# A state-space scan stage: decay rows and their ones held on 128 partitions instead of 2

## The chip, the cores and the metric

The kernel runs as one program on 1 core of one Trainium2 chip. Its time is the device time of an execution in microseconds (us); the profile is of one execution. The engines are TensorE (PE; PEld is its weight load), VectorE (DVE), ScalarE (ACT), GpSimd (POOL) and SyncE (SP, which here issues DMAs).

## What is computed

The kernel is one layer of a diffusion backbone: four parallel branches over 1024 tokens (a conformer convolution, a bidirectional state-space scan, a Hyena branch, a short convolution), merged by gates, and then a mixture of experts. The change lies in the scan branch. Per direction, the reference works over chunks of 128 tokens with 12 heads in 4 groups:

```python
def ssd_scan(xdt, log_decay, b_in, c_out, init):
    xc, a_cum, bc = _ssd_blocks(xdt, log_decay, b_in)
    cc = c_out.reshape(bc.shape).astype(F32)
    h_in, final = _ssd_chunk_states(xc, a_cum, bc, init)
    lower = jnp.tril(jnp.ones((SSD_CHUNK, SSD_CHUNK), dtype=bool))
    decay_in = jnp.exp(jnp.where(lower, a_cum[..., :, None] - a_cum[..., None, :], -jnp.inf))
    cb = jnp.einsum("bclgn,bcsgn->bgcls", cc, bc.astype(F32))
    y_diag = jnp.einsum("bgcls,bgecls,bcsgep->bclgep", cb, decay_in, xc.astype(F32))
    y_off = jnp.einsum("bclgn,cbgepn,bgecl->bclgep", cc, h_in, jnp.exp(a_cum))
    return (y_diag + y_off).reshape(xdt.shape).astype(xdt.dtype), final
```

The two directions are added, with a skip term `xs * ssd_d`. What the change touches is `decay_in`: for every chunk, head and direction a 128x128 table of exp(difference of two cumulated log decays), with one triangle left out.

## The kernel before, in words

`build_program` runs the stages one after another, with a barrier of all engines between them. `stage_scan` has a part of its own for every engine; inside it each engine runs its list in order, and waits on semaphores only. The stage has two parts.

- The early part goes through 11 steps (`early`). In each, SP loads `xs` and `b_tok`, POOL scales them (`ending`, L1346), PE makes a chunk state of four products of 128x192 (`chunk_state`, L1379), and DVE updates the running state (L1491, L1494).
- The loop goes through the 8 chunks, last to first, for both directions together. A chunk has six units `u` of two heads. For each unit PE runs `segments(n, u)`: for either direction a product of the unit matrix `eye` with the table `never` (0, or -1e30 in the forbidden triangle, L1399), and on top of it a product of `ones` with `rows` (L1400). `rows` holds the cumulated log decays in two pieces of fp32r on two partitions, so that L1400 has only 2 rows of contraction; it spreads the sum of the two pieces over all 128 output partitions. ACT takes the exponential (`grow`, L1465, four instructions a unit), and DVE adds the directions (L1501) and multiplies by the scores (L1506): `mix(n, q)`, once for each half `q` of three units.

The other work of a chunk on PE: four products of 128x128 for the scores (L1429), two sets of four of 128x192 with the states (`states_out`, L1407), two sets of six of 128x64 (`diagonal`, L1417) and the next chunk state (L1379). The order on PE in a round is L1429, L1407 (forward), units 3 and 4, L1407 (backward), unit 5, L1417 (half 0), L1379, units 0 to 2 of the next chunk, L1417 (half 1).

What waits for what in the loop: the segments use three PSUM banks in turn, so a unit waits until ACT has read the one three before it (`grown`). DVE's `take_off` (L1512) waits for L1407, and the second L1407 waits for the first L1512 (`off_read`). L1417 of half 0 waits for DVE's L1519 (`y_done`) and for `mix(n, 0)`. L1379 waits for the second L1512. DVE's L1541 waits for L1379, and `mix(n, 1)` stands behind it on DVE. L1417 of half 1 waits for `mix(n, 1)`, and behind it on PE stand L1429 and the first L1407 of the next round. POOL fetches `rows` for the next chunk by two DMAs (L1355), each when PE is done with that half; POOL also computes the skip term (L1367) and `ending`. SP loads the next chunk after `y_done`.

An fp32 product is two records in the profile (so "x8" is four products); an fp32r product is one.

Of the kernel before, what the change touches and what calls it, by code (L numbers as in the profile page):

```python
# [21 lines left out]
F32R = mybir.dt.float32r  # L22
I32 = mybir.dt.int32
ALU = mybir.AluOpType
# [3 lines left out]
P = 128  # L28
# [9 lines left out]
HEADS = 12  # L38
# [856 lines left out]
def ssd_scan_stages(k, merged):  # L895


    with ExitStack() as ctx:
        sb = k.resident(ctx)
        n = CHUNKS + CTX_CHUNKS  # L900
        dt = {name: sb("dt_" + name, [P, n, 2, HEADS]) for name in
              ("exp_cum", "dt_to_end", "total", "bias")}
        stage_ssd_project(k, dt, merged)
        stage_scan(k, dt, merged)
# [343 lines left out]
def stage_scan(k, dt, merged):  # L1248
# [6 lines left out]
    nc, a, ps = k.nc, k.a, k.ps  # L1255
    half, PAIR = SSD_D // 2, 2 * P
    FIRST = 11
    with k.stage("scan") as (sb, sem):
        b_chan, c_chan = sb("b_chan", [P, 2, GROUPS, P]), sb("c_chan", [P, 2, GROUPS, P])
        b_tok, xs = sb("b_tok", [P, 2, GROUPS * P]), sb("xs", [P, 2, SSD_D])  # L1260
        xend = sb("xend", [P, 2, SSD_D])
        rows = sb("rows", [2, 2, HEADS * P], F32R)
        eye, ones = sb("eye", [P, P], F32R), sb("ones", [2, P], F32R)
        never = sb("never", [P, 2, PAIR], F32R)
        grow_f, grow_b = sb("grow_f", [P, 2, HEADS, P]), sb("grow_b", [P, HEADS, P])
        off, skip, state_b = sb("off", [P, SSD_D]), sb("skip", [P, SSD_D]), sb("state_b", [P, 2, SSD_D])
        d_row = sb("d_row", [P, HEADS])
        d_in = sem("d_in")
        in_state, in_out = [sem("in_state0"), sem("in_state1")], [sem("in_out0"), sem("in_out1")]
        in_rows = [sem("in_rows0"), sem("in_rows1")]  # L1270
        skip_ready, rounded, xend_ready, state_mm, state_read = (sem(x) for x in (
            "skip_ready", "rounded", "xend_ready", "state_mm", "state_read"))
# [7 lines left out]
        by_chunk = a["cum_rows"].rearrange("q f (c d h) t -> q (f c) d (h t)", d=2, h=HEADS)  # L1280
        SEG = (0, 1, 7)

        def chunk(n):
            return CHUNKS - 1 - n

        def at(name, c, d, lo=0, hi=HEADS):
            return dt[name][:, c, d, lo:hi]

        def per_head(v, width=HD):
            return v.unsqueeze(2).broadcast_to([P, v.shape[1], width])  # L1290

        def heads(v):
            return v.rearrange("p (h e) -> p h e", e=HD)
# [13 lines left out]
        with nc.Block() as block:  # L1307
            @block.sync
            def _(sp):
                sp.dma_start(d_row[:, :], k.row("ssd_d")).then_inc(d_in, 16)  # L1310

                def load_state(m, c):
                    b = m % 2
                    sp.dma_start(xs[:, b, :], a["xbc_tok"][c, :, 0:SSD_D]).then_inc(in_state[b], 16)
                    sp.dma_start(b_tok[:, b, :], a["xbc_tok"][c, :, SSD_D:SSD_D + GROUPS * P]).then_inc(in_state[b], 16)

                def load_out(n):
                    c = chunk(n)
                    for q, dst in enumerate((b_chan, c_chan)):
                        src = a["xbc_chan"][GROUPS * q:GROUPS * (q + 1), :, c * P:(c + 1) * P]  # L1320
                        sp.dma_start(dst[:, n % 2, :, :], src.rearrange("g p t -> p g t")).then_inc(in_out[n % 2], 16)

                for m, (d, c) in enumerate(early):
                    if m >= 2:
                        sp.wait_ge(state_mm, m - 1)
                    load_state(m, c)
                    if m == 1:
                        load_out(0)
                for n in range(CHUNKS):
                    m = FIRST + n  # L1330
                    if n < 2:
                        sp.wait_ge(state_mm, m - 1)
                    else:
                        sp.wait_ge(y_done, n - 1)
                    load_state(m, chunk(n))
                    if n:
                        load_out(n)

            @block.gpsimd
            def _(pool):  # L1340
                def ending(m, c, d):

                    pool.wait_ge(in_state[m % 2], 32 * (m // 2 + 1))
                    if m >= 2:
                        pool.wait_ge(state_mm, m - 1)
                    nc.gpsimd.tensor_tensor(heads(xend[:, m % 2, :]), heads(xs[:, m % 2, :]),  # L1346
                                            per_head(at("dt_to_end", c, d)), ALU.mult).then_inc(xend_ready, 1)

                for m, (d, c) in enumerate(early):
                    ending(m, c, d)  # L1350
                def load_rows(n, q):
                    if n:
                        pool.wait_ge(seg_mm, 6 * (n - 1) + 3 * q + 3)
                    part = slice(q * half * 2, (q + 1) * half * 2)
                    pool.dma_start(rows[:, :, part], by_chunk[:, chunk(n), :, part]).then_inc(in_rows[q], 16)  # L1355

                pool.wait_ge(d_in, 16)
                load_rows(0, 0)
                load_rows(0, 1)
                for n in range(CHUNKS):  # L1360
                    m = FIRST + n
                    if n + 1 < CHUNKS:
                        load_rows(n + 1, 0)
                    pool.wait_ge(in_state[m % 2], 32 * (m // 2 + 1))
                    if n:
                        pool.wait_ge(y_begun, n)
                    nc.gpsimd.tensor_tensor(heads(skip[:, :]), heads(xs[:, m % 2, :]), per_head(d_row[:, :]),  # L1367
                                            ALU.mult).then_inc(skip_ready, 1)
                    if n + 1 < CHUNKS:
                        ending(m, chunk(n), 1)  # L1370
                        load_rows(n + 1, 1)
# [77 lines left out]
            @block.scalar  # L1449
            def _(act):  # L1450
                nc.scalar.copy(eye[:, :], k.const("ident")).then_inc(rounded, 1)
                nc.scalar.copy(ones[:, :], k.ones[0:2, :]).then_inc(rounded, 1)

                def grow(n, u):
                    act.wait_ge(seg_mm, 6 * n + u + 1)
                    if n >= 2:
                        act.wait_ge(diag_mm, 2 * (n - 2) + u // 3 + 1)
                    if n >= 1:
                        act.wait_ge(summed, 2 * (n - 1) + u // 3 + 1)
                    for d in range(2):  # L1460
                        for e in range(2):
                            h = 2 * u + e
                            dst = grow_b[:, h, :] if d else grow_f[:, n % 2, h, :]
                            at_col = d * PAIR + e * P
                            ins = nc.scalar.activation(dst, ps[:, SEG[(6 * n + u) % 3], at_col:at_col + P], ACT.Exp,  # L1465
                                                       bias=at("bias", chunk(n), d, h, h + 1))
                    ins.then_inc(grown, 1)

                for n in range(CHUNKS):
                    for u in range(6):  # L1470
                        grow(n, u)

            @block.vector
            def _(v):
                ch = Chain(v, dve)
                tt = nc.vector.tensor_tensor
                for d, kept in enumerate(("upto", "from")):
                    nc.vector.tensor_scalar(never[:, d, :].rearrange("p (e t) -> p e t", e=2),
                                            k.const(kept).unsqueeze(1).broadcast_to([P, 2, P]), 1.0, BIG, ALU.subtract,
                                            ALU.mult).then_inc(rounded, 1)  # L1480
# [1484 lines left out]
```

## Time and profile before

| | |
|---|---|
| runs | 2830.58, 2832.65, 2837.83 us; median 2832.65 |
| span of the profiled execution, first to last instruction | 2830.0 us; no other time of that execution is given |
| PE busy | 2510.7 us (89%), 11856 instructions |
| DVE, ACT, POOL busy | 1640.8, 922.9, 380.7 us |
| the scan stage | 857.4 to about 1048.8 us of the span: the early part to 910.8, the loop behind it |
| mean granted TensorE clock, whole span | 0.934 of full speed |

[...] A PE instruction's end is modelled, and consecutive ones overlap in the records, so the interval from start to start tells what one costs in a stream.

### The profile page before, as it was taken

The page shows a single profiled execution, that of the slowest core. Times are in us where ns is not written, and L with a number is a line of the kernel's source. Part 1 is how long each engine was busy: PE and PEld are TensorE (multiplying, and loading weights), DVE is VectorE, ACT ScalarE, POOL GpSimd, SP SyncE. Part 2 cuts the span into 40 slices and gives each one's busy share as a digit, 9 for nine tenths or more (in the row PEclk, how much of TensorE's full clock was granted, in tenths as well). Part 3 has the DMA queues.
Part 4 walks back from the last instruction along what each step waited for, and adds up shares of the span by engine and source line. Part 5 has one row for each costly group of instructions (what it writes and reads, how often), then busy time and mean ns, then how long its engine had stood idle before and what let it go on. Part 6 is the DMA issues. An engine that isn't in the chain of part 4 may idle for free. (4 is left out here: it accounts for less than half of the span.)

```text
span 2830.0 us, 30926 instructions
## 1 busy us (share of the span) xinstructions
PE 2510.7 (89%) x11856; PEld 2008.9 (71%) x11856; DVE 1640.8 (58%) x1613; ACT 922.9 (33%) x1066; POOL 380.7 (13%) x282
## 2 busy tenths in 40 slices
PE   7879967699995999999857999999949999999994
PEld 3338755588874778788745778787838888888881
DVE  4443379533303563332387253566768888888875
ACT  4133300233320433300000010002127777777763
POOL 3210000000003210000332300010001122212210
PEclk9989988899996889999988999999959999999997
DMA  4331144213324112111100111344259999999956
GB/s 171 122 134 45 45 150 141 81 49 99 113 68 157 52 58 73 60 47 47 45 30 30 38 38 45 131 167 159 112 218 359 368 364 365 360 364 390 388 202 241
DMA packets 91342, 433.29 MB, mean 153 GB/s; under 512 B 15864, under 2 KB 25352, under 8 KB 76522
## 3 DMA queue, kind: packets, MB, share of 16 engines
q1 hardware_dynamic: 65194, 355.71, 34.2%
q0 software_dynamic: 26048, 76.20, 7.7%
q8 instruction: 68, 1.11, 0.2%
q14 instruction: 32, 0.26, 0.0%
HBM read 399.41 MB, written 53.41 MB: 160 GB/s over the span
## 5 line engine op out<-in xcount | busy, mean ns | idle before, releaser
L360 PE MATMUL ps<-uT_upper_rest,ring_rest 128*128 128x512 f32 x1360 | 541.6, 398 | 0.0
L360 PEld LDWEIGHTS ps<-uT_upper_rest,ring_rest 128*128 128x128 f32 x1360 | 258.8, 190 | 66.1
L360 PE MATMUL ps<-uT_upper_rest,cs_upper 128*128 128x512 f32 x320 | 130.2, 407 | 55.2 <-DVE cs_val L2076 46.9
L2469 PE MATMUL ps<-ex_u_raw_rest,uT_rest 128*128 128x256 f32 x560 | 156.9, 280 | 0.0
L360 PE MATMUL ps<-uT_upper_rest,xbc_upper 128*128 128x512 f32 x336 | 136.5, 406 | 7.6 <-DVE ring_rest L782 7.6
L2467 PE MATMUL ps<-ring_rest,uT_rest 128*128 128x256 f32 (+1 forms) x416 | 135.1, 325 | 3.1 <-DVE uT_rest L2776 2.4
L360 PE MATMUL ps<-uT_rest,xbc_upper 128*128 128x512 f32 x336 | 134.9, 401 | 0.0
L2467 PE MATMUL ps<-ex_upper,uT_rest 128*128 128x256 f32 (+1 forms) x424 | 134.9, 318 | 0.0
L2468 PE MATMUL ps<-ex_upper,uT_rest 128*128 128x256 f32 (+1 forms) x424 | 134.0, 316 | 0.0
L2468 PE MATMUL ps<-ring_rest,uT_rest 128*128 128x256 f32 (+1 forms) x416 | 133.2, 320 | 0.0
L2366 POOL DMA_INDIRECT y_rows<-sb_uT,ex_scatter_at x35 | 92.6, 2645 | 300.2 <-ACT sb_uT L2575 300.2
L2090 DVE SCALAR_TENSOR_TENSOR sb_y_aT<-cs_val,sb_cols,sb_y_aT 128x64 f32 (+14 forms) x120 | 117.1, 975 | 20.1 <-DVE sb_y_aT L2090 11.7
L360 PE MATMUL ps<-uT_rest,cs_upper 128*128 128x512 f32 x320 | 128.7, 402 | 0.0
L360 PEld LDWEIGHTS ps<-uT_upper_rest,cs_upper 128*128 128x128 f32 x320 | 61.4, 192 | 71.8 <-DVE cs_val L2076 47.4
L2469 PE MATMUL ps<-uT_upper_rest,uT_rest 128*128 128x512 f32 x280 | 110.8, 396 | 0.0
L2469 PE MATMUL ps<-merged_rest,ex_hid_up 128*128 128x512 f32 x280 | 110.8, 396 | 0.0
L2469 PEld LDWEIGHTS ps<-ex_u_raw_rest,uT_rest 128*128 128x128 f32 x560 | 105.3, 188 | 0.0
L1822 PE MATMUL ps<-sb_merged,ring 128*128 128x256 f32 x256 | 64.6, 419 | 34.1 <-DVE sb_merged L1917 34.1
L360 PE MATMUL ps<-uT_upper_rest,hp_upper 128*128 128x512 f32 x192 | 78.3, 408 | 15.8 <-DVE ring_rest L782 15.8
L1986 POOL TENSOR_TENSOR cs_upper<-ring,sb_ones 128x1024 fp32r<-128x1024 f32 x20 | 40.4, 2018 | 380.9 <-POOLq L348 199.7
L2467 PEld LDWEIGHTS ps<-ring_rest,uT_rest 128*128 128x128 f32 x416 | 78.9, 190 | 15.3 <-DVE uT_upper_rest L2625 6.5
L2625 DVE TENSOR_TENSOR uT_upper_rest<-sb_spare,ring_rest 128x2048 fp32r<-128x2048 f32 x36 | 80.9, 2289 | 9.9 <-ACT ring_rest L2552 9.9
(468 smaller groups left out, 6243.6 us busy)
## 6 DMA issues: line engine op xcount, KB each, us to landing
sb_spare<-in_ex_g SPq DMA_DIRECT2D x35, 2048.0 KB
ex_u_raw<-in_ex_u SPq DMA_DIRECT2D x35, 2048.0 KB, 10.4
sb_merged<-in_ex_d SPq DMA_DIRECT2D x35, 2048.0 KB
ring<-in_conv SPq DMA_DIRECT2D x32, 512.0 KB, 3.3
ring<-in_w_gate SPq DMA_DIRECT2D x32, 512.0 KB, 3.3
md_piece<-in_w_late POOLq DMA_DIRECT2D x32, 512.0 KB, 5.1
ring<-in_w_ssd SPq DMA_DIRECT2D x21, 512.0 KB, 3.2
ring<-in_w_mod SPq DMA_DIRECT2D x16, 512.0 KB, 3.3
```

The lines of the kernel that those rows point to most:

```text
L360: last = self.nc.tensor.matmul(out, weight, x[:, k, lo:hi], start=(k == 0 and n == 0), stop=(k == kt - 1 and n == 2))
L1822: mm = nc.tensor.matmul(ps[:, 4 + r, half(mt)], ring.buf[:, slot, at * P:(at + 1) * P], wave[:, h, kt, r, comp, :], start=(kt == 0 and com ...
L1986: ch.step(nc.gpsimd.tensor_tensor(upper[:, slot % 2, :], ring.buf[:, slot, :], k.ones[:, 0:1].broadcast_to([P, KT * P]), ALU.mult))
L2090: ins = nc.vector.scalar_tensor_tensor(out=acc[:, lo:hi], in0=val[:, b, lo + s * GRID_W:hi + s * GRID_W], scalar=tap(i), in1=acc[:, lo:hi] ...
L2366: pool.indirect_dma_start(out=a["y_rows"], out_offset=bass.IndirectOffsetOnAxis(scatter_at[:, i:i + 1], 0), in_=y, in_offset=None, bounds_ ...
L2467: nc.tensor.matmul(out, left_up, w_up, start=first, stop=False)
L2468: nc.tensor.matmul(out, left_lo, w_up, start=False, stop=False)
L2469: return nc.tensor.matmul(out, left_up, w_lo, start=False, stop=last)
L2625: nc.vector.tensor_tensor(chunk(rest, m, b), chunk(raw, m, b), slot(m, b).bitcast(F32), ALU.subtract).then_inc(whole, 1)
```

## The change

`rows` and `ones` get 128 partitions instead of 2. `rows` is written once with zeros by DVE, as its first instruction in the stage (0 times a broadcast of ones, 128x3072 elements). POOL's first DMA into `rows` waits for that (`blank`). The DMAs write the same two partitions as before, so the other 126 stay zero. ACT rounds `ones` on 128 partitions. The products of L1400 are written in the same way, and now contract over 128 rows, of which 126 are zero in the moving operand.

```diff
-        rows = sb("rows", [2, 2, HEADS * P], F32R)
-        eye, ones = sb("eye", [P, P], F32R), sb("ones", [2, P], F32R)
+        rows = sb("rows", [P, 2, HEADS * P], F32R)
+        eye, ones = sb("eye", [P, P], F32R), sb("ones", [P, P], F32R)
...
-        d_in = sem("d_in")
+        d_in, blank = sem("d_in"), sem("blank")
...
-                    pool.dma_start(rows[:, :, part], by_chunk[:, chunk(n), :, part]).then_inc(in_rows[q], 16)
+                    pool.dma_start(rows[0:2, :, part], by_chunk[:, chunk(n), :, part]).then_inc(in_rows[q], 16)
 
                 pool.wait_ge(d_in, 16)
+                pool.wait_ge(blank, 1)
                 load_rows(0, 0)
                 load_rows(0, 1)
...
-                nc.scalar.copy(ones[:, :], k.ones[0:2, :]).then_inc(rounded, 1)
+                nc.scalar.copy(ones[:, :], k.ones[:, :]).then_inc(rounded, 1)
...
                 ch = Chain(v, dve)
                 tt = nc.vector.tensor_tensor
+                nc.vector.tensor_scalar(rows[:, :, :].rearrange("p d (h t) -> p (d h) t", t=P),
+                                        k.ones[:, :].unsqueeze(1).broadcast_to([P, 2 * HEADS, P]), 0.0, None,
+                                        ALU.mult).then_inc(blank, 1)
                 for d, kept in enumerate(("upto", "from")):
```

DVE's list where the stage begins, before the change (the branch is the stage's first entry, `scan_never` the table that is built there, L1486 the first read of a chunk state):

```order
L1473 UNCONDITIONAL_BRANCH
L1478 TENSOR_SCALAR scan_never<-sb_consts 128x256 x2
L1486 COPY sb_merged<-ps 128x768
L1486 COPY scan_state_b<-ps 128x768
L1491 TENSOR_TENSOR sb_merged<-sb_merged,sb_dt_total 128x768
```

And after it, with line numbers higher by 1 to 4:

```order
L1474 UNCONDITIONAL_BRANCH
L1478 TENSOR_SCALAR scan_rows<-sb_ones 128x3072
L1482 TENSOR_SCALAR scan_never<-sb_consts 128x256 x2
L1490 COPY sb_merged<-ps 128x768
L1490 COPY scan_state_b<-ps 128x768
L1495 TENSOR_TENSOR sb_merged<-sb_merged,sb_dt_total 128x768
```

One instruction has come in ahead of the two that build the table. PE has the same instructions in the same order; POOL has the same ones too, its first DMA into `rows` with one wait more.

## Rows read from the trace of the kernel before

**Rows 1.** Page, head.

```profile
span 2830.0 us, 30926 instructions
```

**Rows 2.** Stretches: busy us (instructions) of PE, PEld, DVE, ACT, POOL; PEclk, DMA share, GB/s.

```profile
922.40:1036.10 113.70, 113.70 (x559) 91.22 (x559) 67.97 (x75) 47.89 (x168) 26.39 (x26) 0.91 0.22 65
929.20:932.70 3.50, 3.50 (x14) 2.10 (x12) 2.96 (x4) 1.90 (x7) 0.00 (x0) 0.99 0.00 0
932.70:939.50 6.80, 6.80 (x28) 6.44 (x28) 0.69 (x1) 1.52 (x6) 3.46 (x3) 0.50 0.01 3
983.80:987.20 3.40, 3.40 (x16) 3.40 (x16) 0.00 (x0) 0.25 (x1) 2.85 (x2) 0.50 0.02 4
```

**Rows 3.** Line L1400: durations in ns min/median/max, first and last start, form.

```profile
L1400 PE MATMUL ps<-scan_rows,scan_ones x96: 377/380/578, 911.3 to 1040.8; 2*128 2x256 f32 x96
```

**Rows 4.** PE in order of time, one round at full clock: start, us, what.

```profile
1011.01 1.52 PE L1379 MATMUL ps<-scan_xend,scan_b_tok 128*128 128x192 f32 x8
1012.23 0.41 PE L1399 MATMUL ps<-scan_never,scan_eye 128*128 128x256 f32 x1
1012.58 0.38 PE L1400 MATMUL ps<-scan_rows,scan_ones 2*128 2x256 f32 x1
1012.89 0.38 PE L1399 MATMUL ps<-scan_never,scan_eye 128*128 128x256 f32 x1
...
1016.00 1.55 PE L1417 MATMUL ps<-scan_xs,scan_grow_f 128*128 128x64 f32 x12
1017.39 1.11 PE L1429 MATMUL ps<-scan_c_chan,scan_b_chan 128*128 128x128 f32 x8
1018.34 1.47 PE L1407 MATMUL ps<-sb_merged,scan_c_chan 128*128 128x192 f32 x8
```

**Rows 5.** PE in order of time in the experts' stage.

```profile
2156.51 0.28 PE L2469 MATMUL ps<-ex_u_raw_rest,uT_rest 128*128 128x256 f32 x1
2156.63 0.28 PE L2467 MATMUL ps<-ex_upper,uT_rest 128*128 128x256 f32 x1
```

**Rows 6.** DVE in order of time, the same round as rows 4.

```profile
1004.89 0.96 DVE L1512 TENSOR_TENSOR scan_off<-ps,sb_dt_exp_cum 128x768 f32<-128x768 f32 x1 [5.18 <-PE ps L1407]
...
1007.62 0.95 DVE L1519 TENSOR_TENSOR sb_merged<-sb_merged,ps 128x768 f32<-128x768 f32 x1
...
1009.47 0.96 DVE L1512 TENSOR_TENSOR scan_off<-ps,sb_dt_exp_cum 128x768 f32<-128x768 f32 x1
...
1012.64 0.95 DVE L1541 TENSOR_TENSOR scan_state_b<-scan_state_b,ps 128x768 f32<-128x768 f32 x1 [1.22 <-PE ps L1379]
...
1014.49 0.95 DVE L1506 TENSOR_TENSOR scan_grow_f<-scan_grow_f,ps 128x768 f32<-128x768 f32 x1
...
1019.84 0.96 DVE L1512 TENSOR_TENSOR scan_off<-ps,sb_dt_exp_cum 128x768 f32<-128x768 f32 x1 [3.52 <-PE ps L1407]
```

**Rows 7.** PE in order of time at half clock, and its first segment product.

```profile
910.80 0.58 PE L1399 MATMUL ps<-scan_never,scan_eye 128*128 128x256 f32 x1 [1.12 <-DVE sb_merged L1494]
...
916.92 2.08 PE L1429 MATMUL ps<-scan_c_chan,scan_b_chan 128*128 128x128 f32 x8
918.79 2.77 PE L1407 MATMUL ps<-sb_merged,scan_c_chan 128*128 128x192 f32 x8
...
933.35 2.82 PE L1417 MATMUL ps<-scan_xs,scan_grow_f 128*128 128x64 f32 x12
935.96 2.02 PE L1429 MATMUL ps<-scan_c_chan,scan_b_chan 128*128 128x128 f32 x8
```

**Rows 8.** DVE: the first L1512 of the first and of the last chunk.

```profile
921.59 0.96 DVE L1512 TENSOR_TENSOR scan_off<-ps,sb_dt_exp_cum 128x768 f32<-128x768 f32 x1 [9.74 <-PE ps L1407]
...
1036.49 0.96 DVE L1512 TENSOR_TENSOR scan_off<-ps,sb_dt_exp_cum 128x768 f32<-128x768 f32 x1 [6.09 <-PE ps L1407]
```

**Rows 9.** DVE where the stage begins.

```profile
857.49 0.50 DVE L1478 TENSOR_SCALAR scan_never<-sb_consts 128x256 fp32r<-128x256 f32 x2 [33.77 <-PEq L348]
867.37 0.96 DVE L1486 COPY sb_merged<-ps 128x768 f32<-128x768 f32 x1 [9.38 <-PE ps L1379]
```

## The prediction

> **What bounds the kernel now.** I read the table of stretches over the scan stage first, then PE and DVE in order of time through one round of the loop, then the line of the changed product. The stages run one after another behind barriers, so the stage is judged by itself, and what it gains comes off the total. In the stretch from 922.4 to 1036.1 us PE is busy for all of 113.70 us, and DVE for 67.97, ACT for 47.89 and POOL for 26.39 [rows 2]. The loop is PE's.
>
> Two things there are odd. The first is the clock. It is 0.91 in the mean over that stretch, though PE never stops: it drops to 0.50 for 3.4 or 6.8 us at a time, for instance from 932.7 and from 983.8. The 3.5 us ahead of the first drop hold nothing but segment products, back to back, at 0.99 [rows 2]. The second is the price of a segment product. They start 0.35 and 0.31 us apart at full clock, and last 0.38 us [rows 3, 4]. In the experts' stage, products of the same form on all 128 rows (256 columns, one record each, other weights for each) start 0.12 us apart and last 0.28 us [rows 5]. The only difference in form is that L1399 and L1400 alternate between 128 rows and 2. [...]
>
> From first L1512 of the first chunk to that of the last are 114.90 us for 7 rounds, or 16.41 us each [rows 8]; a round at full clock takes 14.95 us [rows 6]. So the drops cost about 1.46 us a round, 10 us in all.
>
> **The change, part by part.**
>
> *The zeroing.* One DVE instruction of 3072 elements per partition. Two of 256 take 0.50 us [rows 9], at 0.25 to 0.29 us each, so 12 times that is 3.0 to 3.5 us. DVE has been idle there and next has work at 867.37, when `never` was done at 857.99: 9.4 us of cover [rows 9]. POOL's new wait stands ahead of its first DMA into `rows`, needed by the product at 910.80 [rows 7], some 50 us later. Cost zero; if it were not covered, 3.5 us once. ACT's copy on 128 partitions instead of 2 has the same number of elements per partition: zero.
>
> *The segment products, at full clock.* From 0.31 to 0.12 us each. Twelve of them stand before the first L1429, at half clock: 916.92 less 910.80 is 6.1 us, 0.51 each [rows 7]. At twice 0.12 they take 2.9 us. ACT is not in the way, since L1429 doesn't wait for it. That gives 3.3 us once (3.2 or a little more).
>
> In a round there are 24 of them, 7.5 us, which become 2.9. The 4.6 us are not all won, for PE then waits for DVE. PE's own work in a round becomes 2.9 + 2 x 1.39 (L1417) + 0.95 (L1429) + 1.22 (L1379) + 2 x 1.2 (L1407, the form of L1379) = 10.2 us [rows 4]. The chain that then closes the round, with each step from a row and 0.05 us for passing on a wait (an L1407 ends at 1019.81 and L1512 starts at 1019.84):
> - DVE starts L1506 of half 1 at 0, and it ends at 0.95 [rows 6]. Now PE waits for it, which it didn't before; L1417 starts at 1.01.
> - L1417 takes 1.39, L1429 0.95; L1407 starts at 3.35 [rows 4].
> - From L1407's start to L1512's are 1.50 [rows 4, 6]: 4.85.
> - L1512 to the second L1512 on DVE: 4.58 [rows 6]: 9.43. It ends at 10.39; PE starts L1379 at 10.45. (L1417 of half 0 starts after L1519, which begins 2.73 after the first L1512, ends at 8.53, and lets L1417 end by 9.99: 0.46 of slack.)
> - L1379's start to L1541's: 1.63 [rows 4, 6]: 12.08. L1541 to the next L1506: 1.85 [rows 6]: 13.93.
>
> So a round takes 13.93 us at full clock: DVE's operations and PE's by turns. The segments are hidden in it: units 0 to 2 follow L1379, units 3 and 4 lie under L1512, unit 5 under L1501 to L1519. PE waits some 3.7 us a round. ACT's work is 48 us over 7 rounds, under 7 each [rows 2]. The last chunk has no L1379 and no next units, and its end is a row of DVE operations; it stays.
>
> *The clock.* If it never fell, the sum would be 3.3 + 7 x (16.41 - 13.93) = 20.7 us. At half clock everything on PE doubles: a round is then PE's own, 20.4 us (L1417 took 2.61 to the next start and L1429 2.02, twice the value at full clock [rows 4, 7]). With a share s of the loop at half clock the gain is 20.7 - 7 x 6.5 x s. Now s is 0.18 (0.91 in the mean [rows 2]). With that s it is 12.5. Two things pull on s. The drops came behind stretches rich in 2-row products, which suggests that a product on 2 rows hardly counts as activity, and they are gone; but PE now also waits four times a round, for up to 1.8 us, and has fewer columns to stream per us. I take s as it is. Since part of any half-clock time falls on segments with slack around them (1.0 and 1.8 us a round), I take 15, between 12.5 and 20.7 and nearer the lower.
>
> [...]
>
> **Sum.** The profiled execution's span is 2830.0 us [rows 1], 2.65 under the median of 2832.65. 2830.0 - 15 = 2815.0, so 2817.6 as a median of runs.
>
> **Rivals.**
> - *Only the clock is mended.* The 0.31 us have another cause (the fp32r form with these operands), but full-row products keep the clock up. For it: the drops at full PE business. Against: the 0.12 us of the experts' products. Rounds of 14.95: 7 x 1.46 = 10.2, and perhaps 1 to 3 at the start: 2821.
> - *The clock never falls.* The chain of 13.93 with s = 0: 2832.65 - 20.7 = 2812.
> - *Nothing.* The products keep their interval and the clock its drops, since 126 zero rows are no activity, or since the small products of L1417 are what lets it fall. For it: drops also followed stretches with L1417 in them. 2832.65.
> - *Slower: the clock stays down.* PE now idles in each round; before, in the loop, it never did. If the half clock holds for over 20.7 / 45.5 = 45% of the loop, the gain is gone. At two thirds it is 7 x 6.5 x 0.67 - 20.7 = 9.6 us slower: 2842. For it: in the early part, where PE waits most, the clock falls again and again. [...] Against: at half clock PE fills the round by itself (20.4 us) and has no waits left, which is how the clock came back in every case above.
>
> **How the numbers follow.** The likeliest is the new interval with a clock that still falls at times: 0.62, 2817.6, own range 2810 to 2825. The clock alone 0.10, clock never down 0.12, nothing 0.10, slower 0.06. The three runs differ by 7 us, and whatever follows the stage meets the clock's changes at other moments, so 3 to 4 us of scatter lie on each. A measurement can tell about 0.3%, 8.5 us. Faster by that: 0.85 of the likeliest, all of "never down", 0.7 of "clock alone": 0.72. Same: 0.20. Slower: 0.06, with 0.02 for scatter. The range goes from 2808 to 2830: it leaves out the slower case, half of "nothing", and the tails, some 0.18.
>
> **What would show it.** [...] DVE's first L1516 (L1512 before) of the first chunk 3 us earlier relative to the first segment product. Rounds of 13.9 us where the clock is 1.00, with PE waiting for DVE at L1417, L1408 and L1380; if rounds are longer at full clock, I have missed a wait (ACT's `grown`, or the DMA into `rows`). The share of half clock in the loop decides between 2812, 2818 and slower. The zeroing should be over before 862 with nothing behind it late. The prediction is wrong if DVE's operations get slower beside other traffic, or if PE's waits let the clock fall for most of the loop.

## The result and the profile after

| | before | after |
|---|---|---|
| median of 4 runs each, timed side by side | 2834.45 us | 2815.98 us |
| ratio after to before, 95% interval | | 0.9939 [0.9926, 0.9953] |
| span of the profiled execution | 2830.0 us | 2816.3 us |

The gain is 18.5 us by the medians and 13.7 by the two profiled executions; the interval of the ratio is 13 to 21 us. Part of the 18.5 is scatter of the kernel before: its median in a later series of 29 runs on one chip is 2831.6 us. The profiled executions show the gain inside the scan stage. From DVE's first instruction there to the end of its last (0.95 us long) are 857.49 to 1048.82 us before [rows 9 for the begin] and 856.79 to 1033.64 after, which is 14.5 us less.

The rows of the changed kernel follow in the order of those before: the head of the page (against rows 1), the loop from the first chunk's first L1516 to the last chunk's (against rows 2), one stretch of it at half clock, and the changed product (against rows 3).

```profile
span 2816.3 us, 30928 instructions
```

```profile
916.40:1021.20 104.80, 87.36 (x563) 82.31 (x562) 83.54 (x76) 45.72 (x168) 27.29 (x27) 0.92 0.23 70
```

```profile
935.20:938.60 3.40, 3.40 (x13) 3.40 (x14) 1.38 (x2) 0.00 (x0) 0.00 (x0) 0.50 0.90 295
```

```profile
L1401 PE MATMUL ps<-scan_rows,scan_ones x96: 276/282/420, 911.0 to 1023.9; 128*128 128x256 f32 x96
```

PE no longer fills the loop (87.36 of 104.80 us busy), a product on 128 rows lasts 0.28 us instead of 0.38, and the clock still falls: 0.92 in the mean, in five stretches of about 3.4 us. PE in order of time in a round at full clock (against rows 4):

```profile
965.92 1.57 PE L1380 MATMUL ps<-scan_xend,scan_b_tok 128*128 128x192 f32 x8 [0.31 <-DVE scan_off L1516]
967.19 0.41 PE L1400 MATMUL ps<-scan_never,scan_eye 128*128 128x256 f32 x1
967.44 0.28 PE L1401 MATMUL ps<-scan_rows,scan_ones 128*128 128x256 f32 x1
967.56 0.28 PE L1400 MATMUL ps<-scan_never,scan_eye 128*128 128x256 f32 x1
...
970.46 1.55 PE L1418 MATMUL ps<-scan_xs,scan_grow_f 128*128 128x64 f32 x12 [1.54 <-DVE scan_grow_f L1510]
971.85 1.11 PE L1430 MATMUL ps<-scan_c_chan,scan_b_chan 128*128 128x128 f32 x8
972.80 1.47 PE L1408 MATMUL ps<-sb_merged,scan_c_chan 128*128 128x192 f32 x8
```

The interval is 0.12 us. PE now waits where the chain said: 1.54 us for L1510, 0.31 for the second L1516. What has gone is about as long as a weight load. Before, the load of L1400 lasts 0.18 us, starts at 1013.20 together with its own product, and the next load starts only 0.31 us after it; after, a load of 0.19 us starts every 0.12 us, 0.12 ahead of its own product, beside the products before it. First the kernel before, then the one after:

```profile
1013.20 0.18 PEld L1400 LDWEIGHTS ps<-scan_rows,scan_ones 2*128 2x128 f32 x1
1013.51 0.19 PEld L1399 LDWEIGHTS ps<-scan_never,scan_eye 128*128 128x128 f32 x1
```

```profile
967.56 0.19 PEld L1401 LDWEIGHTS ps<-scan_rows,scan_ones 128*128 128x128 f32 x1
967.68 0.19 PEld L1400 LDWEIGHTS ps<-scan_never,scan_eye 128*128 128x128 f32 x1
```

DVE in the same round, then its first and last first-L1516 (against rows 6 and 8), and the beginning of the stage (against rows 9):

```profile
960.33 0.96 DVE L1516 TENSOR_TENSOR scan_off<-ps,sb_dt_exp_cum 128x768 f32<-128x768 f32 x1 [2.41 <-PE ps L1408]
...
964.91 0.96 DVE L1516 TENSOR_TENSOR scan_off<-ps,sb_dt_exp_cum 128x768 f32<-128x768 f32 x1
...
967.60 0.95 DVE L1545 TENSOR_TENSOR scan_state_b<-scan_state_b,ps 128x768 f32<-128x768 f32 x1 [0.74 <-PE ps L1380]
...
969.45 0.95 DVE L1510 TENSOR_TENSOR scan_grow_f<-scan_grow_f,ps 128x768 f32<-128x768 f32 x1
...
974.30 0.96 DVE L1516 TENSOR_TENSOR scan_off<-ps,sb_dt_exp_cum 128x768 f32<-128x768 f32 x1 [0.77 <-PE ps L1408]
```

```profile
856.79 1.76 DVE L1478 TENSOR_SCALAR scan_rows<-sb_ones 128x3072 fp32r<-128x3072 f32 x1 [33.93 <-PEq L348]
...
866.61 0.96 DVE L1490 COPY sb_merged<-ps 128x768 f32<-128x768 f32 x1 [7.66 <-PE ps L1380]
...
916.36 0.96 DVE L1516 TENSOR_TENSOR scan_off<-ps,sb_dt_exp_cum 128x768 f32<-128x768 f32 x1 [4.74 <-PE ps L1408]
...
1021.17 0.96 DVE L1516 TENSOR_TENSOR scan_off<-ps,sb_dt_exp_cum 128x768 f32<-128x768 f32 x1 [5.62 <-PE ps L1408]
```

This round takes 974.30 - 960.33 = 13.97 us. The seven rounds are 13.11, 15.26, 15.60, 13.97, 15.63, 13.97 and 17.27 us, 14.97 in the mean against 16.41. The zeroing takes 1.76 us and DVE then waits for PE as before.

From the first segment product to the first L1516 it was 921.59 - 910.80 = 10.79 us [rows 7, 8]; it is 5.78:

```profile
910.58 0.58 PE L1400 MATMUL ps<-scan_never,scan_eye 128*128 128x256 f32 x1 [1.11 <-DVE sb_merged L1498]
...
913.30 1.72 PE L1430 MATMUL ps<-scan_c_chan,scan_b_chan 128*128 128x128 f32 x8
914.86 1.47 PE L1408 MATMUL ps<-sb_merged,scan_c_chan 128*128 128x192 f32 x8
```

Twelve products take 2.72 us instead of 6.12 (3.4 won), and from L1430's start to L1516's it is 3.06 us instead of 4.67 (1.6 won): L1408 lasts 1.47 us instead of 2.77, at full clock, and L1430 1.72 instead of 2.08, at full clock for a part, where both ran at half [rows 7]. So the account is 5.0 at the start and 7 x 1.44 = 10.1 in the rounds, 15.1; 0.6 us of it are missing in the stage's 14.5, mostly since the first segment product starts 0.5 us later counted from the stage's beginning.

### The profile page after: what moved, and what is told of

The parts are those of the page before. It is cut to its first block and busy times, and to the rows that moved or that the text cites. A ratio compares the mean times of both kernels' runs of the same rounds, so it can differ in the third digit from the quotient of the medians.

```text
span 2816.3 us, 30928 instructions
## 1 busy us (share of the span) xinstructions
PE 2477.2 (88%) x11856; PEld 1997.4 (71%) x11856; DVE 1656.8 (59%) x1614; ACT 920.6 (33%) x1066; POOL 381.3 (14%) x282
## 5 line engine op out<-in xcount | busy, mean ns | idle before, releaser
L360 PE MATMUL ps<-uT_upper_rest,ring_rest 128*128 128x512 f32 x1360 | 541.8, 398 | 0.0
L360 PEld LDWEIGHTS ps<-uT_upper_rest,ring_rest 128*128 128x128 f32 x1360 | 259.3, 191 | 66.3
L360 PE MATMUL ps<-uT_upper_rest,cs_upper 128*128 128x512 f32 x320 | 130.2, 407 | 55.0 <-DVE cs_val L2080 46.8
L360 PE MATMUL ps<-uT_upper_rest,xbc_upper 128*128 128x512 f32 x336 | 136.5, 406 | 7.6 <-DVE ring_rest L782 7.6
L360 PE MATMUL ps<-uT_rest,xbc_upper 128*128 128x512 f32 x336 | 134.9, 401 | 0.0
L360 PE MATMUL ps<-uT_rest,cs_upper 128*128 128x512 f32 x320 | 128.9, 403 | 0.0
L360 PEld LDWEIGHTS ps<-uT_upper_rest,cs_upper 128*128 128x128 f32 x320 | 61.4, 192 | 71.6 <-DVE cs_val L2080 47.2
L360 PE MATMUL ps<-uT_upper_rest,hp_upper 128*128 128x512 f32 x192 | 78.2, 408 | 15.8 <-DVE ring_rest L782 15.8
```

The costliest lines, as they stand in the source:

```text
L360: last = self.nc.tensor.matmul(out, weight, x[:, k, lo:hi], start=(k == 0 and n == 0), stop=(k == kt - 1 and n == 2))
```

## The experiments

Each was compared with the kernel before on the same chip. The lines shown are of one execution of each. Three theories were at stake: **A**, the 0.19 us too much are paid each time PE goes from a product on 128 rows to one on 2 or back, and perhaps for other pairs of row counts; **C**, the clock holds with products on many rows, zeros or not, and falls with products on few; and **the chain**, a round is now DVE and PE by turns, 13.93 us at full clock.

**1. The zeroing alone.** Tensors and zeroing as after, but the product reads two rows:

```diff
-ones[:, :], rows[:, d, u * PAIR:(u + 1) * PAIR]
+ones[0:2, :], rows[0:2, d, u * PAIR:(u + 1) * PAIR]
```

> The kernel after, with rows and ones still on 128 partitions and zeroed once, but the product of L1401 reads two partitions of each again. Theory A (the gain comes from products that no longer alternate between 2 and 128 rows): interval of the segment products 0.31 us again, rounds of 14.95 us at full clock, time that of before, 2834 us, within 0.3%. Rival (the gain came from where the tensors lie, or from the shift of the stage against the rest): stays near 2816. The zeroing itself costs under 0.5 us in both.

Ratio 1.0004 [0.9989, 1.0019]; the rounds at full clock are 14.95 us again. The whole gain is in the product's rows; where the tensors lie and the zeroing do nothing that can be measured.

**2 and 3. 64 rows and 96 rows.** The same edit with `0:64` and with `0:96`.

> As after, but the products of L1401 contract over 64 partitions (62 of them zero). [...] For the clock, if rows count as activity, 64 rows give half of a full product, so fewer drops to half clock in the loop than before (20 us of it): 5 to 12 us; the time is 2824 to 2832. Rival B (the extra time belongs to very few rows, as 2): interval 0.12 us, time about 2816.

> As after, but the products of L1401 contract over 96 partitions. [...] Rival (any difference of the row count between neighbours costs): interval 0.31 us, time 2824 to 2834.

By theory A, I put 64 rows with 2 (an interval of 0.31 us, rounds of 14.95 us at full clock) and 96 with 128 (0.12 us, rounds of 13.97, a time of 2816 within 0.3%). That grouping was a guess; no run had shown it.

64 rows: ratio 0.9997 [0.9983, 1.0011], no gain; 96 rows: 0.9952 [0.9937, 0.9967]. The lines of the product in the two kernels:

```profile
L1401 PE MATMUL ps<-scan_rows,scan_ones x96: 379/382/579, 912.8 to 1040.7; 64*128 64x256 f32 x96
```

```profile
L1401 PE MATMUL ps<-scan_rows,scan_ones x96: 278/283/420, 911.7 to 1027.7; 96*128 96x256 f32 x96
```

A product lasts 0.38 us with 64 rows, as with 2, and 0.28 with 96, as with 128. So it is not any difference in the row count that costs: beside products on 128 rows, 2 and 64 are dear (0.31 us from start to start at full clock) and 96 is not (0.12). What I expected of the clock with 64 rows was wrong, and the time lies above the range that I gave: the loop has 0.92 in the mean, hardly better than the 0.91 before. That is taken up in 8. With 96 rows the profiled execution has 0.87 over its loop, less than the 0.92 of the kernel after, at the same intervals; so how often the clock falls is not settled by the interval alone.

**4. Half as many changes, the same columns, 2 rows.** On the kernel before:

```diff
-                    for d in range(2):
-                        out = ps[:, at_bank, d * PAIR:(d + 1) * PAIR]
-                        nc.tensor.matmul(out, eye[:, :], never[:, d, :], start=True, stop=False)
-                        mm = nc.tensor.matmul(out, ones[:, :], rows[:, d, u * PAIR:(u + 1) * PAIR], start=False, stop=True)
+                    out = ps[:, at_bank, 0:2 * PAIR]
+                    nc.tensor.matmul(out, eye[:, :], never[:, :, :], start=True, stop=False)
+                    mm = nc.tensor.matmul(out, ones[:, :], rows[:, :, u * PAIR:(u + 1) * PAIR], start=False, stop=True)
```

> The kernel before (2 rows), but both directions of a unit go in one product of 512 columns for the table and one of 512 for the rows: half as many products, half as many changes between 128 and 2 rows, the same columns. Theory A (0.19 us for each change): 0.42 us a product instead of 2 x 0.31, so 0.84 us a unit instead of 1.25; PE then waits for DVE and the round at full clock is that of the chain, 13.9 to 14.0 us. At the start 1.2 us are won instead of 3.3. The 2-row products still count little for the clock, which has more of them per column worked: half clock for 20 us or more of the loop. Time 2818 to 2828. Rival (the extra time grows with the columns, as two passes would): 0.6 us a product, time as before, 2834.

PE in order of time, at full clock:

```profile
918.61 0.50 PE L1399 MATMUL ps<-scan_rows,scan_ones 2*128 2x512 f32 x1
919.04 0.50 PE L1398 MATMUL ps<-scan_never,scan_eye 128*128 128x512 f32 x1
919.47 0.49 PE L1399 MATMUL ps<-scan_rows,scan_ones 2*128 2x512 f32 x1
```

0.43 us apart: twice the columns add 0.12 us to the 0.31. Products of 512 columns that all are on 128 rows start 0.23 us apart at full clock (L360 in the same execution, at 1149.61, 1149.84 and 1150.07), so the extra here is 0.20 us a product, beside 0.19 with 256 columns. The 0.43 are theory A's 0.42 to 0.01, and from 256 to 512 columns the extra hardly grew. Rounds of 14.07, 14.06 and 13.95 us came where the clock held, the chain's own. Yet the ratio is 0.9992 [0.9972, 1.0012], no gain, and the median of 2829.1 us lies just outside my range. The runs go from 2813 to 2839 us, and their mean granted clock over the whole span goes with them, from 0.938 in the fastest to 0.929 in the slowest. In the profiled one, at 2822 us of span, the loop from first L1511 (the L1516 of this kernel) to last had 0.89 against 0.91 before, and three rounds of 16.5 to 17.15 us at its start. What the fewer changes gave was for the most part lost again to the clock.

By the records the price is about a weight load that is not hidden: 0.18 to 0.19 us of load and 0.12 for 256 columns make 0.30 to 0.31, against 0.31; with the 0.23 for 512 columns they make 0.41 to 0.42, against 0.43; and at half clock the load lasts 0.28 to 0.29 us, which with the 0.21 of a stream of one kind (run 8) makes 0.49 to 0.50, against 0.51. Those sums are my estimate; why the load is not hidden at such a change, no run shows.

**5. Products to fill the wait.** On the kernel after, behind units 0 to 2 of the next chunk, into a part of a bank that nobody reads:

```diff
                             segments(n + 1, u)
+                        for _ in range(8):
+                            nc.tensor.matmul(ps[:, 4, half:half + P], eye[:, :], never[:, 0, 0:P], start=True, stop=True)
                     diagonal(n, 1)
```

> As after, but 8 full products of 128 columns stand ahead of the diagonal products of half 1, where PE waits 1.2 to 1.6 us for DVE in each round; nobody reads them. They take 0.9 us at full clock and should fit in the wait. Theory C: more activity, so fewer drops to half clock in the loop (after: five of 3.4 us in the profiled run, rounds of 14.97 us in the mean against 13.97 at full clock); if all go the mean is 13.97 and 7 us are won: 2809 to 2816. Rival (the fillers delay the diagonal products, or the drops come from elsewhere): 2816 or more.

Ratio 0.993 [0.9912, 0.9948], median 2811.6 us. The loop in one stretch:

```profile
915.40:1013.60 98.20, 86.77 (x619) 82.13 (x618) 82.74 (x75) 45.74 (x168) 28.12 (x27) 0.98 0.25 75
```

The clock is 0.98 instead of 0.92, the rounds 13.11, 15.17, 13.97, 13.97, 13.97, 13.98, 14.03: 98.2 us in all, 6.6 less than after. So the half-clock stretches of the changed kernel cost some 7 us, and PE's waits have a part in them: with useless products in one of the waits, one long round was left, of 15.17 us, where there were four of 15.26 to 17.27. The 6.6 us are between two profiled executions; the intervals of the two ratios overlap.

**6. The forward states earlier.** On the kernel after; `forward_states` is the wait for the loads and the states with `states_out(n, 0)`, taken from behind the scores:

```diff
                             segments(n + 1, u)
+                        forward_states(n + 1)
                     diagonal(n, 1)
```

> As after, but the product of the next chunk's forward states (L1408, first set) stands ahead of the diagonal products of half 1 instead of behind the scores. It takes L1418, L1430 and L1408 out of the chain between DVE's L1510 and its next L1516. By the chain as I read it, DVE is then bound by itself: L1510, L1528, L1516. If L1528 keeps the 3.2 us that it takes now beside POOL's two products, L1516 starts 4.2 us after L1510 instead of 4.85: rounds of 13.3 us at full clock. If it took its own 0.95 us it would be 11.0. I expect the first, with somewhat fewer drops in clock: 2806 to 2813. Rival (the chain is another one): rounds stay at 13.97, time at 2816.

Ratio 0.9905 [0.9888, 0.9923], median 2805.2 us; the rounds are 13.69, 14.73, 13.10, 13.10, 13.09, 13.11, 13.82. That is 13.1 us where I expected 13.3, and the median is 0.8 us under my range. The chain was the bound, and DVE's L1528 beside POOL came in where I put it. The clock over these rounds is 0.96.

**7. The same move in the kernel before.**

> The same move of L1407 in the kernel before (2 rows). There PE is busy in all of the loop, so the order doesn't matter: rounds of 14.95 us at full clock, and time within 0.3% of before. Rival (something else than PE sets the round before): 2 us or more are won in each round, 2815.

A miss: ratio 1.0065 [1.0036, 1.0094], slower by 18 us (10 to 27). A round of 14.95 us occurs, so at full clock the order did not matter, as expected; but the clock did. In the profiled execution it stayed at half for 20.5 us on end, and one round took 24.46 us:

```profile
997.10:1017.60 20.50, 20.50 (x68) 16.99 (x66) 8.07 (x9) 3.87 (x14) 3.62 (x4) 0.50 0.19 59
```

PE is busy for all of it by the record. Why the clock stays down longer here is open. L1417, L1429 and the first L1407 still follow one another without segment products between them, only with L1407 in front instead of behind; before, the clock came back by the end of that piece in the stretch from 932.7 us [rows 2]. No run tests what in the order decides it.

**8. Streams of one kind.** On the kernel after, behind the last chunk, streams of products of 256 columns into a bank nobody reads, in one execution. Two of them, as written:

```diff
+                for _ in range(120):
+                    nc.tensor.matmul(spare, ones[0:2, :], rows[0:2, 0, 0:PAIR], start=True, stop=True)
...
+                for _ in range(30):
+                    nc.tensor.matmul(spare, eye[:, :], never[:, 0, :], start=True, stop=True)
+                    nc.tensor.matmul(spare, ones[0:96, :], rows[0:96, 0, 0:PAIR], start=True, stop=True)
```

> As after, and behind the last chunk PE runs streams of products of 256 columns whose results nobody reads: 120 full (128 rows), then 120 each on 2, 32, 64, 96 and 128 rows of the mostly zero decay rows, with 80 full ones between, and then five streams in which two kinds alternate, 30 pairs each: 128 and 2 rows, 128 and 96, 128 and 64, 32 and 2, 64 and 2. Output as before. [...] Rival B (few rows are dear by themselves): the stream on 2 rows also runs at 0.31. For the clock, theory C (rows in use count as activity, zeros or not): it falls to half in the streams on 2 and 32 rows though PE is never idle, and holds in those on 96 and on 128 rows; 64 is open. Rival D (only time busy counts): it holds in all of them. Rival E (nonzero data count): it falls in the stream on 128 mostly zero rows too.

By theory A, I put a stream of one kind at 0.12 us a product at full clock whatever its rows, the alternations of 128 with 2, 128 with 64 and 64 with 2 at 0.31, and those of 128 with 96 and 32 with 2 at 0.12.

The streams by stretches: 2, 32, 64, 96 and 128 rows, then 128 and 2 alternating, and 128 and 64:

```profile
1050.00:1069.00 19.00, 19.00 (x91) 18.96 (x89) 0.00 (x0) 0.00 (x0) 0.00 (x0) 0.50 0.00 0
1084.50:1104.00 19.50, 19.50 (x94) 19.50 (x93) 0.00 (x0) 0.00 (x0) 0.00 (x0) 0.50 0.00 1
1118.00:1130.00 12.00, 12.00 (x102) 12.00 (x101) 0.00 (x0) 0.00 (x0) 0.00 (x0) 1.00 0.00 0
1141.00:1154.00 13.00, 13.00 (x111) 13.00 (x110) 0.00 (x0) 0.00 (x0) 0.00 (x0) 1.00 0.00 1
1165.00:1178.00 13.00, 13.00 (x111) 13.00 (x110) 0.00 (x0) 0.00 (x0) 0.00 (x0) 1.00 0.00 1
1183.00:1205.00 22.00, 22.00 (x45) 12.34 (x44) 0.00 (x0) 0.00 (x0) 0.00 (x0) 0.50 0.00 0
1221.00:1242.00 21.00, 21.00 (x42) 11.79 (x42) 0.00 (x0) 0.00 (x0) 0.00 (x0) 0.50 0.00 0
```

A stream on 2 or on 32 rows runs at the same interval as a full one (34 products on 2 rows in the 4 us before the clock fell, and 26 on 32 rows in 3 us, 0.12 each; 0.21 at half clock), and its clock then falls to 0.50 though PE never stops. On 64, 96 and 128 rows it stays at 1.00, the last with 126 rows of zeros: zeros alone didn't lower it. Alternating 128 and 64 rows, both of which hold 1.00 alone, goes with 0.50 (0.51 us a product there, against 0.21 without changes), and 128 with 96 doesn't: entered at 0.50 with 0.21 us a product, it came back to 1.00 and 0.12 us at 1210.4. Alternating 32 and 2 rows costs nothing extra (0.21 us a product at half clock), 64 and 2 does (0.51):

```profile
1242.79 0.41 PE L1481 MATMUL ps<-scan_rows,scan_ones 32*128 32x256 f32 x1
1243.00 0.41 PE L1482 MATMUL ps<-scan_rows,scan_ones 2*128 2x256 f32 x1
```

```profile
L1485 PE MATMUL ps<-scan_rows,scan_ones x30: 575/575/575, 1255.8 to 1285.2; 2*128 2x256 f32 x30
```

So of the five pairs tried three are dear when they alternate, 128 with 2, 128 with 64 and 64 with 2, and two are not, 128 with 96 and 32 with 2. For the drops of the clock before the change two things come into question, few rows and the alternation. The alternation is enough, as run 2 shows with 64 rows: 0.92 over the loop with PE busy for all of 115.40 us, though 64 and 128 rows each hold 1.00 alone. Whether the 2 rows added to it, no run shows.

**9 and 10. Past the changed kernel.** On run 6: DVE's L1528 moved from in front of the first L1516 to behind the second; then, on top, SP asks for `b_chan` and `c_chan` of the next chunk when PE is done with them (`off_mm`), ahead of its wait for `y_done`.

> As states_early, and DVE's L1528 (scaling of the backward state, which waited 3.2 us beside POOL's two products there) stands behind the second L1516 instead of in front of the first. If an operation that reads PSUM isn't held by POOL, L1516 starts 1 us after L1510 instead of 4; the next one on SBUF alone, L1505, is then held until POOL is done, to 4.0. L1510, L1523, L1536 and the second L1516 follow at 4.1, 4.9, 5.8, 6.8; L1380 at 7.8; the next L1510 at 11.3, plus up to 1 us of waiting for c_chan. Rounds of 11.3 to 12.3 us at full clock against 13.10, 2793 to 2800. Rival (POOL holds every DVE operation, or L1505 is held as long as L1528 was): rounds of 12.9 or more, 2803 to 2806.

> As dve_order, and SP asks for b_chan and c_chan of the next chunk as soon as PE is done with them, ahead of y_done, and not behind it. In states_early PE waited 0.9 us a round for c_chan. If that wait lies on the chain of dve_order, 0.3 to 1 us a round go: 2 to 7 us. Rival (the wait is hidden behind DVE): same as dve_order within 0.1%.

Run 9: ratio 0.9873 [0.9846, 0.99], median 2794.7 us, rounds of 11.60 to 11.85 us but for the first two. Run 10: 0.9863 [0.9839, 0.9888], 2791.1 us, rounds of 11.36 to 11.39 but for the first, of 9.45. The intervals of the two overlap, and those of runs 6 and 9 just do, so these steps show in the rounds more surely than in the times. DVE of run 10 at the start of a round, and POOL beside it:

```profile
953.96 0.96 DVE L1523 TENSOR_TENSOR scan_off<-ps,sb_dt_exp_cum 128x768 f32<-128x768 f32 x1
954.83 2.27 DVE L1512 TENSOR_TENSOR scan_grow_f<-scan_grow_f,scan_grow_b 128x768 f32<-128x768 f32 x1
957.14 0.95 DVE L1517 TENSOR_TENSOR scan_grow_f<-scan_grow_f,ps 128x768 f32<-128x768 f32 x1
```

```profile
953.37 1.49 POOL L1370 TENSOR_TENSOR scan_skip<-scan_xs,scan_d_row 128x768 f32<-128x768 f32 x1
954.80 1.48 POOL L1348 TENSOR_TENSOR scan_xend<-scan_xs,sb_dt_dt_to_end 128x768 f32<-128x768 f32 x1
```

The operation that reads PSUM takes its 0.96 us while POOL works on its first product and the start of its second; the one on SBUF alone ends 0.82 us after POOL's, 1.3 us late. In run 10 this repeats from round to round, with 0.82 or 0.83 us. DVE is now the bound (76.67 of 77.70 us). PE waits 3.2 us of these 77.70 in run 10, 7.2 us of 81.00 in run 9, and the clock is 1.00 over the loop in both; in the kernel after PE waits 17.4 of 104.80 us and the clock is 0.92.

## Why the prediction was right

- **What bounds the loop, and the two oddities.** Right: PE, at an interval of 0.31 us that was not the products' own. Runs 1 to 4 and 8 show the change between 128 rows and 2 or 64 as the cause; in a stream of one kind the interval at full clock is 0.12 us on 2, 32, 64, 96 and 128 rows alike (run 8). The records show a weight load that is not overlapped: 0.18 to 0.19 us, started together with its own product before and 0.12 us ahead of it after, beside the 0.19 us that went. What else PE does at such a change, and why, is not shown.
- **The zeroing.** Nothing, under cover. It took 1.76 us and not 3.0 to 3.5; the price from an instruction of 256 elements was too high for one of 3072. ACT's copy took 0.29 us on 128 partitions as on 2.
- **The start.** Predicted 3.3 for the products; measured 3.4. I left out that the clock also comes back sooner, which gave 1.6 more.
- **The chain of 13.93 us.** Measured 13.97, step by step as listed: L1516 to the second 4.58, L1380's start to L1545's 1.68 instead of 1.63. The waits of PE stand where they were put. The first round is shorter, 13.11 us, since the first chunk has no L1523; that was left out. Runs 5 and 6 confirm it by moving it.
- **The clock.** Its share at half was taken as it was, 0.18; it was 0.16 (0.92 in the mean). The price was taken wrongly in two ways. First, the formula multiplies by rounds, while 0.18 is a share of time; as a share of time, a stretch of 3.4 us would cost 3.4 x (20.4 - 13.93) / 20.4 = 1.1 us by the two round times. It cost 1.6: the rounds are 7.9 us longer than without the five stretches. The formula's 45.5 x 0.16 = 7.3 us comes near that only by the mix-up. Second, 1.6 is nearly half of 3.4, so the slack around the segments, for which I rounded 12.5 up to 15, gave hardly anything. The sum closes another way: 20.7, plus 1.6 at the start, plus 0.8 for the first round, less 7.9, is 15.2, against the 15.1 measured. The 15 was right by luck, as errors cancelled. (L1429's 2.02 us, called twice its value, is a duration beside an interval of 0.95; its interval at half clock is 1.87 us [rows 7]. Nor does everything on PE double at half clock: L1429 goes from 0.95 to 1.87 us and L1417 from 1.39 to 2.61, a segment product of the kernel after from 0.12 to 0.21.) And I held the 2 rows for what pulled the clock down; with 64 rows, which alone hold it at 1.00 (run 8), it fell nearly as much, to 0.92 in the mean against 0.91.
- **The sum.** 2817.6 predicted, 2815.98 measured, in the likeliest case's own range. Of the gain, 15 were predicted and 14.5 measured in the stage; the median's 18.5 holds scatter.

Of the rivals, "only the clock is mended" and "nothing" fell with the interval. "The clock never falls" is what run 5 came near to, and 9 and 10 reached with other chains. "Slower" did not come. Run 7 shows that half clock held for 20.5 us on end in this loop, but in the kernel before, with alternating products and PE busy, and not through the waits that this rival was about.

What I missed in the trace is DVE's L1528: it takes 3.2 us in the median and up to 3.55, where it took 0.95, since it now meets POOL's products; moved away from them in run 9, it took 0.95 again. It ends 0.8 us before the next L1516 can start, and so cost nothing, but it was next in line.

## What to carry to other kernels

Compare the start-to-start interval of a product with that of the same form elsewhere in the trace: here 0.19 of 0.31 us went into changes between products on 2 and on 128 rows, with PE busy all the while. Padding the small operand once with rows of zeros, to 96 or 128 rows, brought the interval to 0.12 us; the zeroing took 1.76 us, all hidden. That ended PE's rule over the loop here (87.36 of 104.80 us busy), and the next gains, to 2805.2, 2794.7 and 2791.1 us in runs 6, 9 and 10, came from the chain between the engines. With the changes gone, the clock was higher where the waits were shorter or filled: 0.92 over the loop after, 0.98 in run 5, 1.00 in runs 9 and 10.

## What the runs showed of the hardware that I had not expected

- The granted clock fell to 0.50 in an unbroken stream of products on 2 or 32 rows, and stayed at 1.00 on 64, 96 and 128 rows, zeros or not (run 8, one execution).
- Alternating products on 128 and 64 rows fell to 0.50, though each kind alone kept 1.00 (run 8); in the loop with 64 rows the clock was 0.92, with PE busy throughout (run 2).
- Half clock lasted with PE busy throughout: 20.5 us in a loop in which products on 128 and 2 rows alternate for much of the time (run 7), and 22 us of nothing but alternation in run 8.
- A DVE product of SBUF operands that met POOL's products ended 0.8 us after POOL's last, and took up to 3.55 us for 0.95 (kernel after); one with an operand in PSUM took its 0.96 us beside POOL (run 10).
